# Sliding-window attention, recurrence and its norm interleaved in one stage, and the background transposes dealt out anew

## The reference, cut to what matters

```python
def hybrid_layer(x, ...):
    h = rms_norm(x, norm_mix_g)
    aq, ak, av, hq, hf, hi, hg, ga, gh = split_combined(h @ w_in)
    y_attn = sliding_window_attention(aq, ak, av, sinks)    # 8 heads of 64, 2 kv heads, window 128
    o = hgrn2_recurrence(silu(hq), hf, hi, lower_bound)      # 4 heads of 128x128 state, chunks of 32
    o = rms_norm(o, hgrn_norm_g) * silu(hg)                  # mean over the 128 features of a head
    merged = sigmoid(ga) * (y_attn @ w_attn_proj) + sigmoid(gh) * (o @ w_hgrn_proj)
    x = x + merged @ w_out
    return x + peer_layer(rms_norm(x, norm_ffn_g), w_peer_q, peer_keys, peer_u, peer_v)

def sliding_window_attention(q, k, v, sinks):
    # per block of 128 queries: scores with the block and the one before it, ALiBi bias,
    # p = softmax(scores and one sink per head)[..., :-1];  out = p @ v
    ...

def hgrn2_recurrence(q, f_logit, i, lower_bound):
    # b = cumsum of log f within a chunk; q_dec = q*exp(b); k_inv = k*exp(-b)
    # a = causal(q_dec @ k_inv);  ds = (k*exp(b_last-b)) @ v;  state = exp(b_last)*state + ds
    # o = a @ v + q_dec @ state_before_the_chunk
    ...
```

## Time and profile before

| | us |
|---|---|
| median of three runs (2431.86 to 2433.99) | 2431.93 |
| the profiled execution | 2441.25 |
| its span in the trace | 2439.4 |

### The profile page before, as it was taken

The page is one execution under the profiler, slowest core; times in us unless marked ns, Lnnn a source line. Parts: engine busy times, 40 slices in busy tenths (PEclk is TensorE's granted clock), DMA queues, the critical chain, the costliest instruction groups (busy, mean ns, idle before and its releaser), DMA issues. The chain is left out here.

```text
span 2439.4 us, 24361 instructions
## 1 busy us (share of the span) xinstructions
PE 2082.1 (85%) x8036; PEld 1395.9 (57%) x8036; DVE 1564.6 (64%) x3433; ACT 484.1 (20%) x1053; POOL 844.0 (35%) x637
## 2 busy tenths in 40 slices
PE   5998869697978989999988989888766579989977
PEld 4765848565826976556555555555422257724445
DVE  4468654436999975666666666666777776346752
ACT  3344032112211320000000000000000221334541
POOL 3420024323300005666555455444676232300002
PEclk8998579898988999999999999999988789989999
DMA  7875849974564559999999999999999321100001
GB/s 274 323 280 192 311 157 364 344 272 164 205 234 163 210 213 401 402 402 402 402 403 403 404 402 402 402 402 402 402 400 402 152 92 61 52 22 1 1 35 69
DMA packets 203900, 648.09 MB, mean 266 GB/s; under 512 B 19840, under 2 KB 52736, under 8 KB 202496
## 3 DMA queue, kind: packets, MB, share of 16 engines
q1 hardware_dynamic: 118384, 335.60, 37.4%
q0 software_dynamic: 73728, 268.47, 27.9%
q10 hardware_dynamic: 11664, 42.47, 5.1%
HBM read 560.48 MB, written 85.98 MB: 265 GB/s over the span
## 5 line engine op out<-in xcount | busy, mean ns | idle before, releaser
L1527 PE MATMUL ps<-arena 128*128 128x512 f32 x1024 | 516.8, 652 | 143.2 <-DVE arena L1384 99.6
L1395 DVE CUSTOM_DVE_ANT_0 arena<-arena 128x1024 bf16<-128x1024 f32 x256 | 313.3, 1224 | 249.1 <-DMA arena<-u_rows,u_row 138.2
L1516 PE MATMUL ps<-rows_n,arena 128*128 128x256 f32 x2048 | 465.5, 380 | 0.0
L1516 PEld LDWEIGHTS ps<-rows_n,arena 128*128 128x128 f32 x2048 | 387.4, 190 | 95.7 <-issue 49.5
L1527 PEld LDWEIGHTS ps<-arena 128*128 128x128 f32 x1024 | 206.7, 208 | 398.9 <-issue 261.4
L1259 POOL DMA_INDIRECT arena<-u_rows,u_row x256 | 291.7, 1140 | 312.6 <-DMA gates<-arena 169.0
L1259 POOL DMA_INDIRECT arena<-in_v,expert x192 | 213.3, 1111 | 312.3 <-DVE arena L1416 283.3
L1416 DVE SCALAR_TENSOR_TENSOR arena<-arena,wt 128x1024 f32<-128x1024 f32 x192 | 246.2, 1282 | 0.4
L188 DVE STREAM_TRANSPOSE tdst<-tsrc 128x1024 f32<-128x1024 f32 x128 | 156.6, 1234 | 138.2 <-DMA u_rows<-tdst 137.7
L1493 ACT ACTIVATE ge<-dots 128x2 f32<-128x2 f32 x128 | 26.0, 203 | 906.3 <-DVE dots L1395 906.3
L232 POOL TENSOR_TENSOR in_wlo<-in_raw,in_whi 128x1024 fp32r<-128x1024 f32 x45 | 113.7, 2529 | 231.9 <-ACT in_whi L228 231.9
(11 more groups left out here) (388 smaller groups left out, 3002.2 us busy)
## 6 DMA issues: line engine op xcount, KB each, us to landing
tsrc<-in_u SPq DMA_DIRECT2D x128, 512.0 KB, 6.8
u_rows<-tdst SPq DMA_DIRECT2D x128, 512.0 KB, 4.7
arena<-in_u SPq DMA_DIRECT2D x128, 512.0 KB, 10.6
arena<-in_v SPq DMA_DIRECT2D x128, 512.0 KB, 11.8
in_raw<-in_panels ACTq DMA_DIRECT2D x37, 512.0 KB, 3.8
gates<-arena SPq DMA_DIRECT2D x8, 2048.0 KB, 8.8
arena<-gates SPq DMA_DIRECT2D x32, 512.0 KB, 18.8
mg_raw<-in_panels ACTq DMA_DIRECT2D x28, 512.0 KB, 6.6
```

The costliest lines, as they stand in the source:

```text
L1395: nc.vector.tensor_tensor_reduce(out=junk[:, n % 2], in0=u_slot[n % NU], in1=hrows[:, n // NPICK], scale=1.0, scalar=0.0, op0=ALU.mult, op ...
L1516: mm = nc.tensor.matmul(ps[:, j % 2, 0:TD], ud[:, j % RJ, k], rows_n2[:, 0, k], start=k == 0, stop=k == KD - 1)
L1527: mm = nc.tensor.matmul(ps[:, 4 + 2 * t + c], park[:, j % NPK, t * P:(t + 1) * P], vd[:, j % RJ, c * T:(c + 1) * T], start=j == 0, stop=j ...
```

## The change

The turns become 38 in in1, 28 in a joint stage, 38 in mg, 4 in n2, 20 in pq (128 as before). In the joint stage attention's 32 jobs run as before, and in every second job stands one chunk of the recurrence; in every eighth a tile is finished: its output copied and squared by ScalarE, its mean taken by TensorE, its root, gain and gate by ScalarE and VectorE, and its two output parts written. The last tile's norm stays in the stage hn. VectorE still scales the probabilities; the sink and the sign are taken in one instruction from sinks negated once. Scores have three banks, and the transposes, the value products, the matrix `a` with the turned keys, `ds`, and the output have one each. Turned keys are written over `kk`, four states are kept for eight, and `bB` shares the memory of `kinv`, so that the exponentials in in1 also wait for "b last - b". A strided copy `e_last` keeps the chunks' decays. In mg the turns stand at listed places: four behind the first gate of each of the first six column blocks, none in the seventh, two in the eighth, and two behind each of the first six out projections.

```diff
-TURNS = 30, 14, 20, 46, 2, 16
+TURNS = 38, 28, 38, 4, 20
...
-    bB = sb(b1b, "bB", [P, HG, T])
+    bB = kinv
+    eb = sb(b1b, "eb", [P, HG, T])
...
+        nc.vector.tensor_copy(e_last[:].rearrange("p h c -> p (h c)"), flat(eb)[:, :, CHUNK - 1])
         nc.vector.tensor_tensor(hq[:], hq[:], eb[:], ALU.mult)
...
-    specs += [own("exps", "act", both_exps, "b"),
+    specs += [own("exps", "act", both_exps, "b", "b last - b"),
...
-        attention_stage("wa", jobs, units, 2, T_WA, (sinks_loaded, 16))
+        SCORE, TURN, PV, AM, DS, OUT = (0, 1, 2), 3, 4, 5, 6, 7
+        chunk_at = {2 * c: c for c in range(NC_)}
+        tile_at = lambda i, x: (i - x) // 8 if i >= x and (i - x) % 8 == 0 and (i - x) // 8 < NT - 1 else None
...
+            def scores(i):
+                if i >= 3:
+                    pe.wait_ge(S["exp"], i - 2)
...
+            def turned(j):
+                pe.wait_ge(S["prob"], j + 1)
+                if j:
+                    pe.wait_ge(S["copied"], j)
...
+            def out(t):
+                pe.wait_ge(S["am"], t + 1)
+                if t:
+                    pe.wait_ge(S["y"], t)
+                pe.wait_ge(S["stt"], 4 * t + 3)
...
+            def mean(t):
+                pe.wait_ge(S["of"], t + 1)
+                pe.wait_ge(S["sq"], t + 1)
...
+            keys_turned(0)
+            within(0)
+            for i in range(n + 4):
+                if i < n:
+                    scores(i)
+                if 3 <= i < n + 3:
+                    turned(i - 3)
+                if i - 4 in last_job:
+                    pv(last_job.index(i - 4))
+                if tile_at(i, 7) is not None:
+                    mean(tile_at(i, 7))
+                if i in chunk_at:
+                    c = chunk_at[i]
+                    if c < NC_ - 1:
+                        added(c)
+                    if c % 4 == 2 and c // 4 + 1 < NT:
+                        keys_turned(c // 4 + 1)
+                    if c % 4 == 3:
+                        if c // 4 + 1 < NT:
+                            within(c // 4 + 1)
+                        out(c // 4)
...
+            def next_state(c):
+                v.wait_ge(S["ds"], c + 1)
+                if c:
+                    v.wait_ge(S["stt"], c)
+                if c % 4 == 3:
+                    v.wait_ge(S["o"], c // 4 + 1)
...
+            for j in range(n + 4):
+                if j < n:
+                    largest(j)
+                if 1 <= j <= n:
+                    inverse(j - 1)
+                if j in chunk_at and chunk_at[j] % 4 == 0:
+                    masked(chunk_at[j] // 4)
+                for x in range(turn_in[j]):
+                    turner.turn(v)
+                if j - 4 in last_job and last_job.index(j - 4) % 2:
+                    unit_out(last_job.index(j - 4) // 2)
+                if j in chunk_at and chunk_at[j] < NC_ - 1:
+                    next_state(chunk_at[j])
+                if tile_at(j, 8) is not None:
+                    normed(tile_at(j, 8))
+                if tile_at(j, 10) is not None:
+                    low(tile_at(j, 10))
...
+            for j in range(n + 4):
+                if j < n:
+                    exps(j)
+                if 3 <= j < n + 3:
+                    copied(j - 3)
+                if j in chunk_at and chunk_at[j] % 4 == 2 and chunk_at[j] // 4 + 1 < NT:
+                    keys_out(chunk_at[j] // 4 + 1)
+                if j % 8 == 7 and j // 8 < NT:
+                    tile_out(j // 8)
+                if tile_at(j, 8) is not None:
+                    act.wait_ge(S["mean"], tile_at(j, 8) + 1)
+                    seed_tile(tile_at(j, 8), ps[:, OUT]).then_inc(S["seed"], 1)
...
-    NC_ = T // CHUNK
-    with ExitStack() as st:
-        tok = sb(st, "kdec_tok", [P, HG, NT, P])
...
-            nc.scalar.activation(sq[:], hf[:], ACT.Square).then_inc(S["sq"], 1)
...
+            nc.scalar.activation(kinv[:, :, t * P:], hf[:, :, t * P:], ACT.Square).then_inc(S["sq"], 1)
+            act.wait_ge(S["mean"], 1)
+            seed_tile(t, ps[:, 0]).then_inc(S["seed"], 1)
+            act.wait_ge(S["y"], 1)
+            high_tile(t).then_inc(S["hi"], 1)
             for i in range(2):
                 mg_weights.make_hi(act, i)
...
-        mms = list(range(5 * KD - 2))
-        panel_stage("mg", PAN["merge"], with_side(specs, lambda u, s: turns_after(u, mms, T_MG)), weights=mg_weights)
+        places = [4 * m for m in range(KD - 2) for x in range(4)] + [4 * KD - 4] * 2 + [4 * KD + m for m in range(KD - 2) for x in range(2)]
+        panel_stage("mg", PAN["merge"], with_side(specs, lambda u, s: sum(turns_after(x, range(len(places)), T_MG)
+                                                                          for x, y in enumerate(places) if y == u)),
```

More of the change, by code:

```diff
@@ L779, in program, with seed_tile, norm_tile, high_tile @@
         return
+    def seed_tile(t, bank):
+        return nc.scalar.activation(kinv[:, :, t * P:(t + 1) * P], bank.rearrange("p (h s) -> p h s", h=HG), SEED, bias=cst("eps"))
+    def norm_tile(chain, t, mean):
+        s = slice(t * P, (t + 1) * P)
+        root(chain, kk[:, :, s], mean, kinv[:, :, s], kk[:, :, s])
+        chain(nc.vector.scalar_tensor_tensor(out=hf[:, :, s], in0=hf[:, :, s], scalar=vec("hgrn_norm_g"), in1=kk[:, :, s],
+                                             op0=ALU.mult, op1=ALU.mult))
+        return nc.vector.tensor_tensor(hg[:, :, s], hg[:, :, s], hf[:, :, s], ALU.mult)
+    def high_tile(t):
+        s = slice(t * P, (t + 1) * P)
+        return nc.scalar.activation(y_hi[:, 4:8, s], hg[:, :, s], ACT.Copy)
+    def low_tile(t):
+        s = slice(t * P, (t + 1) * P)
+        return nc.vector.tensor_tensor(y_lo[:, 4:8, s], hg[:, :, s], y_hi[:, 4:8, s].bitcast(F32), ALU.subtract)
     with ExitStack() as st:
@@ new lines, in program @@
+        mx = sb(st, "wh_mx", [P, 4, 4])
+        rs = sb(st, "wh_rs", [P, 4, 4])
+        neg_sinks = sb(st, "wh_neg_sinks", [P, HEADS])
+        state = sb(st, "state", [P, NST, HG, P])
+        at = sb(st, "hgrn_a", [P, HG, P])
+        tok = kk
+        names = ("scores negmax exp sinkexp prob turned copied pv unit dve zero "
+                 "kturned tok a am ds stt o of sq mean seed y hi lo")
+        S = dict(zip(names.split(), sems(st, " ".join("wh_" + x for x in names.split()))))
+        block = st.enter_context(nc.Block())
@@ L820, in program @@
         return
-    NC_ = T // CHUNK
-    with ExitStack() as st:
-        tok = sb(st, "kdec_tok", [P, HG, NT, P])
[L826 to L902, removed]
-                for h in range(HG):
-                    mm = nc.tensor.matmul(ps[:, 4 + c % 2, h * P:(h + 1) * P], tok[r, h, t], hv[r, h, t], start=True, stop=True)
-                mm.then_inc(S["ds"], 1)
[L907 to L910, removed]
-                pe.wait_ge(S["stt"], 4 * t + 3)
-                for h in range(HG):
-                    bank = ps[:, 6 + t % 2, h * P:(h + 1) * P]
-                    nc.tensor.matmul(bank, hv[:, h, t], at[:, t % 2, h], start=True, stop=False, skip_group_check=True)
-                    for c in range(4 * t, 4 * t + 4):
-                        if c:
-                            s = slice(CHUNK * (c % 4), CHUNK * (c % 4) + CHUNK)
-                            mm = nc.tensor.matmul(bank[:, s], state[:, c % NST, h], hq[:, h, c * CHUNK:(c + 1) * CHUNK],
-                                                  start=False, stop=c % 4 == 3, skip_group_check=True)
-                mm.then_inc(S["o"], 1)
-            amat(0)
-            for c in range(NC_):
-                if c < NC_ - 1:
-                    ds(c)
-                if c % 4 == 1 and c // 4 + 1 < NT:
-                    amat(c // 4 + 1)
-                if c % 4 == 3:
-                    out(c // 4)
@@ L934, in program @@
     with ExitStack() as st:
[L935 to L936 removed]
+        t = NT - 1
+        names = ("sq mean seed y hi lo dve").split()
         S = dict(zip(names, sems(st, " ".join("hn_" + x for x in names))))
```

177 lines of the change are left out of this document (152 added, 25 removed).

## The result

The changed kernel takes **2472.53 us** (median of 4 runs, 2463.99 to 2475.33), the kernel before, on the same chip, 2432.96 (2431.86 to 2438.74): ratio 1.0152, 95% interval 1.0121 to 1.0182. It is slower, by 39.6 us; the forecast was 2419.7, range 2402 to 2445.

The account below looks back on a forecast made before the run. Each stage had its own bound: TensorE in in1, VectorE in wa and pq, a wait for `m_lo` stalling mg. Terms +12 - 10 - 22 + 3 + 4.8 = -12.2 took 2431.93 to 2419.7 us, range 2402 to 2445.

Parts of the forecast that it names:

- term for VectorE: Joint stage: the list of VectorE's own work there, summed to 112.0 us.
- covered at 0.78: Joint stage: TensorE's own work, 84 us at 2.4 GHz, stays hidden at a clock of 0.78 (108).
- three tile waits: Joint stage: VectorE waits three times for an output tile, 10 us at high clock, 28 at low, 17 taken.
- clock test I gave: Joint stage: the forecast counts as wrong if TensorE's clock there is under 0.6.
- start and end: Joint stage: VectorE's waits at its two ends, taken from wa as 10.1 us.
- Place (2): Joint stage: after a tile, TensorE computes mean and next scores only behind ScalarE's work; VectorE waits three times, 7.5 us.
- low-clock rival: Joint stage: the recurrence's products pull the clock down, TensorE bounds; 190 us with hn, total 2449; chance 0.15.
- The clock stays high: Rival, mainly joint stage: scores hold TensorE at 2.4 GHz, so waits shrink; -29 in all, total 2403; chance 0.20.
- in1: First stage: eight more turns at 3.0 us, up to 12.0 absorbed by VectorE's idle time; +12, ends +8 and +20.
- mg: Stage mg: listed turn places cut the 23.95 us wait for the last `m_lo` to 2.7; -22, ends -23 and -10.
- n2: Stage n2: two more turns ahead of a root; +3, between 1 and 5.
- The turns' rival: Turns cost more than places hide: in1 +20, mg saves 15, n2 +5; +5 in all, total 2437; chance 0.13.

Follow-up runs that it names:

- wide_products_4: The changed kernel with four wide bf16 products added ahead of each job's scores in the joint stage; 2446.51 us (one run).
- copy_before_exp: The changed kernel with ScalarE copying out the transpose of job j-3 before, not after, the exponential of job j; 2460.57 us, ratio 1.0125.
- joint_old_turns: The changed kernel with the turns of the kernel before (30, 34, 46 spread evenly in mg, 2, 16); 2461.65 us, ratio 1.0108.
- turns_alone: The kernel before, not interleaved, with the changed kernel's deal of turns (38, 14, 14, 38, 4, 20); 2441.91 us, ratio 1.0046.
- fewer_wide: The kernel before with turns 30, 22, 20, 38, 2, 16 and four wide products ahead of each chunk's ds in hg; 2441.95 us, ratio 1.0024.

## Why the prediction was wrong

**The joint stage**, the step that failed. Its term for VectorE was near (104.75 for 112.0). What failed is "covered at 0.78": I carried wa's clock over to a stage that is half recurrence. The three tile waits were then 29.1 us for 17. My two prices for them were right: 28 at the low clock (0.61 here), 10 at the high one (10.8 at 0.89 in `wide_products_4`). I had read hg's 0.50 at 8.00 of 8 us busy and used it for a rival only. The clock test I gave (wrong if under 0.6) was passed by a hair, at 0.61, while the stage was 25 us off: below 0.7, as that rival said, nothing is saved.

A second term was mis-sized, the start and end "as in wa", 10.1. They took 20.5: 7.0 at the start, and at the end 7.63 and 5.89 behind the fourth output tile, on which I had put no price. Place (2) was right, 3.19 + 2.22 + 2.58 = 8.0 us for 7.5. The 8.9 us of idle time left are short waits and gaps, for which I had nothing.

Behind these waits stands a path that I had seen and not priced. I had written that TensorE's transpose stands behind ScalarE's copy, and that behind an exponential. I took VectorE's norm as a cover for ScalarE's table loads; in truth the loads and then the norm delay the maximum, the exponential, the copy and so TensorE, three times by 5.8 us. VectorE is at work meanwhile, but TensorE reaches its next tile later. `copy_before_exp` gives the price, 10.7 us: the tile waits are 23.8 there for 29.1, those for scores 19.7 for 23.6.

The low-clock rival, at 190 for joint and hn, was the nearest: 184.5 measured. I had given it 0.15. TensorE was not busy throughout, as it had it, but 143.65 of 171.2 us. "The clock stays high" was wrong in this kernel. By the Trainium skill (TensorE: Matmul & The Clock Gate, "What's actually happening") activity releases the throttle. Hg, with a stretch of 8.00 of 8 us busy at 0.50, and its 0.95 once wide products were added, say that the bare busy share of the records does not decide it.

**in1**, +18.5 for +12. The direction of the mechanism was right, its price too low. On the marks of the table, VectorE's work grew by 9.1 us and its waits for the store by 19.3 (72.8 for 53.5), 28.4 where I had 8 x 3.0 = 24.0. I gave VectorE's other idle time credit for up to 12 us; 9.8 of it was used up. One late copy on VectorE (L478), behind two turns that had waited for a store, held TensorE for 12.6 us at once, 1.4 before, and TensorE's clock over the stage went from 0.99 to 0.94. It lies in my range of 8 to 20. `e_last` took 1.56 us, and 0.18 in `joint_old_turns`, whose in1 is 0.4 us longer than before's; under 0.3, as I had it, holds where GpSimd does not work beside it (see the last heading).

**mg**, 24.0 to 5.0 where I had 24.0 to 2.7. The places work. The rest is one instruction: the cast to `m_hi` took 2.61 us, 0.43 before. It began with an instruction of GpSimd and ended 0.28 us after it; the last heading has the other cases. Mg as a whole came out at 188.3 for 205.4, -17.1 for -22, within my ends.

**n2**, +6.5 for +3 (ends 1 and 5): the third and fourth turn each waited for a store, 4.43 + 1.26 us, ahead of the root. I took the middle since the queue has few panels there, but with two buffers the third of four turns in a row waits for the first one's store. **pq**, +6.6 for +4.8: VectorE is the bound as said, and two turns also waited 3.8 us for stores there. **hn**, 13.3 for 14, was right.

**The turns' rival** (2437) was near with its in1 price, 20 for 18.5; but mg saved more than its 15.

**Sum to the expert stage**: +28.5 for -12.2. Behind it the two executions differ by 5.0 us more. The medians differ by 39.6, since the profiled execution of before was 8.3 us above the median of 2432.96, and that of after 1.8 above its own.

## What to carry to other kernels

Before two chains are interleaved, write the lists of all engines side by side and follow each single buffer back through them: an instruction that frees a bank must not stand in its engine's list behind one that waits for a long step elsewhere. And take TensorE's clock from the stage whose products the new stage has, not from the busier one; where the merged stage has long tiles of short products, price them at the low clock. A background task should go where its engine has idle time and its data has a free queue: here a turn cost from 0.95 us (joint stage) to 3.3 (n2) by its place alone, for 1.17 of work, and 1.6 in wa and 1.65 in pq, which VectorE bounds.

## What was not expected of the hardware

**Work that does nothing can pay for itself.** 128 extra 128x512 bf16 products made the joint stage and hn 17.6 us shorter. In hg, 120 of them took 28.4 us and lifted TensorE's clock from 0.55 to 0.95 without costing time.

**An instruction of VectorE can last as long as one of GpSimd beside it.** In mg the cast to `m_hi` takes 0.43 us and `m_lo` 0.69. In the traces of before and after, one of the two is long, 2.56 to 2.77 us, in ten of the sixteen pairs. Each of the ten runs beside GpSimd's L232 and ends 0.3 to 0.6 us after it; the other six pairs have no such neighbour. With the new places of the turns the pairs start in step with GpSimd, eight of eight, where before it was two. The copy `e_last` shows the same: 0.18 us alone, 1.56 beside L232. The turns' transposes take their 1.25 us beside it as alone. This is read from the traces; no kernel was built to test it.

**A stage behind the change has two lengths.** "All behind" varied between 1747.6 and 1761.6 us over kernels that are the same there, in one profiled execution of each. The difference sits in the first 15 us or so of the second layer's attention. Here is that stretch, in the kernel before and in `turns_alone`:

```profile
2179.40:2199.40 20.00, 19.06 (x43) 6.97 (x43) 9.29 (x37) 8.65 (x24) 0.00 (x0) 0.57 0.00 1
```

```profile
2179.80:2199.80 20.00, 18.88 (x59) 6.86 (x58) 14.18 (x46) 11.27 (x28) 0.00 (x0) 1.00 0.00 1
```

TensorE is at full clock ahead of it, pauses for 0.9 us, and in some executions then runs at 0.50 for some 15 us. Of the fourteen profiled executions it was slow in seven, those of before and after among them. "All behind" was 1759.2 us in these on the average and 1749.8 in the others, about 9 us less. So one profiled span of this kernel is good to 9 us only, and stages have to be compared, not spans. What decides it was not found. Executions without a profile leave no trace, but if one kernel starts slow there more often than another, its median moves by several us with its stages unchanged. That would fit `fewer_wide`, 7.0 us above before with equal stages up to there, `joint_old_turns` above its range, and the 39.6 us between the medians for 28.5 in the stages; it is not shown.
